# Sums of squares multiplied with a tile of 128 columns instead of a constant of two

## What is computed

```python
def rms_norm(x, g):
    xf = x.astype(jnp.float32)
    y = xf * lax.rsqrt(jnp.mean(xf * xf, axis=-1, keepdims=True) + EPS)
    return (y * g.astype(jnp.float32)).astype(x.dtype)

def first_block(x, ...):
    for layer in range(DEPTH):
        hn = rms_norm(x, norm_mix_g[layer])
        ...
        x = x + mix
        x = x + sq_relu_mlp(rms_norm(x, norm_mlp_g[layer]), mlp_w_up[layer], mlp_w_down[layer])
    return rms_norm(x, final_norm_g)
```

## Time and profile before

| | us |
|---|---|
| median of 3 runs | 850.53 (850.45 to 850.67) |
| the profiled execution | 849.28 |
| its span, first to last instruction | 847.5 |
| TensorE busy, matmuls | 842.2 |
| VectorE busy | 647.2 |
| ScalarE busy | 505.9 |
| GpSimd busy | 46.8 |

### The profile page before, as it was taken

The page is one execution under the profiler, slowest core; times in us unless marked ns, Lnnn a source line. Parts: engine busy times, 40 slices in busy tenths (PEclk is TensorE's granted clock), DMA queues, the critical chain, the costliest instruction groups (busy, mean ns, idle before and its releaser), DMA issues.

```text
span 847.5 us, 17537 instructions
## 1 busy us (share of the span) xinstructions
PE 842.2 (99%) x7184; PEld 822.4 (97%) x7184; DVE 647.2 (76%) x1229; ACT 505.9 (60%) x925; POOL 46.8 (6%) x63
## 2 busy tenths in 40 slices
PE   8999999999999999999999999999999999999998
PEld 7999999999999998999999999999999999999998
DVE  6978668898987697586667555566699889998873
ACT  5795777774435567578878444434456685444650
POOL 0000000000000127100000000021020000000000
PEclk9999999999999999999999999999999999999999
DMA  9927868788887824177757865526564424556541
GB/s 300 347 70 224 276 213 264 265 281 267 299 263 233 283 72 140 51 247 237 208 174 217 242 207 189 189 71 154 172 198 151 148 77 142 156 170 192 170 144 50
DMA packets 162865, 164.23 MB, mean 194 GB/s; under 512 B 16816, under 2 KB 159328, under 8 KB 162528
## 3 DMA queue, kind: packets, MB, share of 16 engines
q1 hardware_dynamic: 161696, 162.05, 60.6%
q10 hardware_dynamic: 1088, 1.05, 0.4%
HBM read 162.01 MB, written 2.91 MB: 195 GB/s over the span
## 4 chain that ended last, share of the span: by engine, by line
PE 97%; DVE 1%; DMA 1%; ACT 0%; SPq 0%; POOL 0%; issue 0%
PE ps L316 25%; PE ps L318 25%; PE ps L320 25%; PE ps L442 3%; PE ps L1594 2%; PE ps L1592 2%; PE ps L1596 2%; PE ps L459 2%; PE ps L1685 1%; PE ps L1687 1%; PE ps L1689 1%; PE ps L1643 1%; PE ps L1654 1%; PE ps L1634 1%; DMA raw<-in_rec_w_in_dram 1%; PE ps L1133 1%
## 5 line engine op out<-in xcount | busy, mean ns | idle before, releaser
L283 DVE TENSOR_TENSOR wl<-raw,wh 128x1024 fp32r<-128x1024 f32 x256 | 309.1, 1223 | 27.1 <-ACT wh L276 27.0
L316 PE MATMUL ps<-xh,wh 128*128 128x256 f32 x1136 | 319.1, 281 | 0.0
L318 PE MATMUL ps<-xl,wh 128*128 128x256 f32 x1136 | 315.1, 277 | 0.0
L320 PE MATMUL ps<-xh,wl 128*128 128x256 f32 x1136 | 315.0, 277 | 0.0
L276 ACT ACTIVATE wh<-raw 128x1024 fp32r<-128x1024 f32 x256 | 267.1, 1051 | 73.7 <-PE ps L320 66.0
L316 PEld LDWEIGHTS ps<-xh,wh 128*128 128x128 f32 x1136 | 213.3, 188 | 3.1 <-issue 1.2
L318 PEld LDWEIGHTS ps<-xl,wh 128*128 128x128 f32 x1136 | 213.8, 188 | 0.4 <-DVE xl L384 0.2
L320 PEld LDWEIGHTS ps<-xh,wl 128*128 128x128 f32 x1136 | 213.8, 188 | 0.0
L320 PE MATMUL ps<-hh,wl 128*128 128x256 f32 x512 | 141.3, 276 | 0.0
L316 PE MATMUL ps<-hh,wh 128*128 128x256 f32 x512 | 141.3, 276 | 0.0
L318 PE MATMUL ps<-hl,wh 128*128 128x256 f32 x512 | 141.3, 276 | 0.0
(11 more groups left out here) (365 smaller groups left out, 1396.4 us busy)
## 6 DMA issues: line engine op xcount, KB each, us to landing
raw<-in_w_in_dram SPq DMA_DIRECT2D x34, 1024.0 KB, 5.4
raw<-in_mlp_up_dram SPq DMA_DIRECT2D x32, 1024.0 KB, 5.5
raw<-in_mlp_down_dram SPq DMA_DIRECT2D x32, 1024.0 KB, 7.1
aw<-in_w_adaT_dram SPq DMA_DIRECT2D x24, 512.0 KB, 4.7
raw<-in_rec_w_in_dram SPq DMA_DIRECT2D x7, 1024.0 KB, 11.6
raw<-in_att_w_in_dram SPq DMA_DIRECT2D x6, 1024.0 KB, 5.5
raw<-in_rec_w_out_dram SPq DMA_DIRECT2D x4, 1024.0 KB, 5.9
raw<-in_att_w_o_dram SPq DMA_DIRECT2D x4, 1024.0 KB, 5.0
```

The lines of the kernel that those rows point to most:

```text
L283: e.tensor_tensor(parts_of(i)[1], raw_of(i), f32(parts_of(i)[0]), op=ALU.subtract).then_inc(S["wl"], 1)
L316: e.matmul(o, H[:, first + n], xh[:, k], start=start and n == 0, stop=False)
L318: e.matmul(o, H[:, first + n], xl[:, k], start=False, stop=False)
L320: ins = e.matmul(o, L[:, first + n], xh[:, k], start=False, stop=stop and n == len(ks) - 1)
```

## The change

The moving operand of the sums becomes ONES, a new tile of 128 x 128 filled with 1/1024 by GpSimd at the start, at an address of its own behind the other tiles. The first sum waits for that tile instead of the table, and the first spread, which reads the identity, gets the wait for the table. The results take 128 columns of a PSUM bank each where they took two; VectorE reads the first column of each.

```diff
+    ONES = place("ones", [128, 128], at=[228480])
...
     def rms_sum_pe(e, q, r):
         p = claim(q, AUX[0], (S["var"], r + 1))
         q.wait_ge(S["sqa"], 7 * (r + 1))
-        q.wait_ge(S["con"], 16)
-        e.matmul(p[:, 0:2], SQA[:, 0:128], cc("i1024"), start=True, stop=True)
-        e.matmul(p[:, 2:4], SQA[:, 128:256], cc("i1024"), start=True, stop=True).then_inc(closing(f"sum{r}", p), 1)
+        q.wait_ge(S["negh"], 2)
+        e.matmul(p[:, 0:128], SQA[:, 0:128], ONES[:], start=True, stop=True)
+        e.matmul(p[:, 128:256], SQA[:, 128:256], ONES[:], start=True, stop=True).then_inc(closing(f"sum{r}", p), 1)
 
     def rms_spread_pe(e, q, r):
         p = claim(q, AUX[1], (S["rs"], r + 1))
         q.wait_ge(S["rst"], r + 1)
+        q.wait_ge(S["con"], 16)
...
-        e.tensor_scalar(VAR, ps[f"sum{r}"][:, 0:4:2], EPS, None, op0=ALU.add).then_inc(S["var"], 1)
+        e.tensor_scalar(VAR, ps[f"sum{r}"][:, 0:256:128], EPS, None, op0=ALU.add).then_inc(S["var"], 1)
...
-                ins = e.matmul(p[:, 4 * i + 2 * b:4 * i + 2 * b + 2], acc[:, b * 128:b * 128 + 128], cc("i1024"),
+                ins = e.matmul(p[:, 256 * i + 128 * b:256 * i + 128 * b + 128], acc[:, b * 128:b * 128 + 128], ONES[:],
                                start=True, stop=True)
...
-        e.tensor_scalar(FV[:, 0:2], ps["fsum"][:, 0:4:2], EPS, None, op0=ALU.add).then_inc(S["fv"], 1)
+        e.tensor_scalar(FV[:, 0:2], ps["fsum"][:, 0:256:128], EPS, None, op0=ALU.add).then_inc(S["fv"], 1)
         q.wait_ge(S["fv"], 1)
-        e.scalar_tensor_tensor(FV[:, 2:4], FV[:, 0:2], EPS, ps["fsum"][:, 4:8:2], op0=ALU.mult,
+        e.scalar_tensor_tensor(FV[:, 2:4], FV[:, 0:2], EPS, ps["fsum"][:, 256:512:128], op0=ALU.mult,
                                op1=ALU.add).then_inc(S["fv"], 1)
...
             e.memset(NEGH[:], -0.5).then_inc(S["negh"], 1)
+            e.memset(ONES[:], 1.0 / 1024).then_inc(S["negh"], 1)
             e.memset(XRP[:, :, 0:3], 0.0).then_inc(S["pad"], 1)
```

## The result

| | before | changed |
|---|---|---|
| median, us | 850.60 (850.45 to 850.94) | 861.63 (861.15 to 862.70) |
| runs | 4 | 4 |
| span of the profiled execution, us | 847.5 | 859.6 |

The ratio is 1.0130, with a 95% interval of 1.0116 to 1.0143: 11.0 us slower. The forecast was 850.6 us, within 0.2% of no change, with a range of 849.5 to 851.8 and 0.05 for a loss over 0.2%. It was wrong.

What follows compares the result with a forecast made beforehand. The prediction took TensorE, on the chain for 97% of the span at full clock, as the bound. Matmuls 0.05, later sums 0 and memset with waits 0 were added to the 850.53 us median: 850.6 us, range 849.5 to 851.8.

Steps and rivals of the forecast that it cites:

- Part 1: The 28 fp32 passes of the sums: widening the moving operand from 2 to 128 columns adds only 0.05 us.
- rows 2: Trace rows around the 2-column sum in the norm ahead of the first MLP: 98.67 to 99.35, 0.68 us.
- rows 4: Trace rows around the final norm's eight passes with 2 columns: 552.13 to 553.25, 1.12 us.
- rows 3: Trace rows around the 128-column spread, two products after the first MLP's norm sum: 104.76 to 105.45, 0.69 us.
- The 0.08 us are given back at once: Inside a sum's group: the second call starts 0.08 us later, the next ordinary matmul follows that much sooner.
- rival B: At six sum groups the later starts are not given back: 0.08 us each remain, 0.48 us, 851.0 us; chance 0.08.
- Part 2: Behind the sums: each lands 0.11 us later, but idle time of its readers covers this; cost 0, at most 0.66 us.
- Part 3: Program start: GpSimd's new memset and the moved wait for the constants cost 0; without cover at most 0.31 us.
- A: At all 28 passes the columns are paid in full on top of the weight load: 853.5 us; chance 0.04.
- C: At the first sum, constants ordinarily land last and the sum is now free of them: up to -0.43 us, 850.1; chance 0.05.
- D: No set place: new tile's position or a shifted program start moves time beyond 0.2%; chance 0.03 (0.02 faster, 0.01 slower).

## Why the prediction was wrong, point by point

**What bounds the kernel.** Right: TensorE at the full clock, with no idle time. But "busy" was read as a fixed amount of work. The same matmuls take 113.3 or 117.8 ns each, and neither the busy share nor the clock tells which.

**Part 1, the price of the 28 passes: right as far as it went.** Forecast 0.68 to 0.70 us for the stretch of rows 2, measured 0.68; forecast 1.12 for that of rows 4, measured 1.13. The Trainium skill's rule for isolated matmuls (TensorE: Matmul & The Clock Gate, "Back-to-back issue gap"), by which the 28 passes would have cost 0.87 us more, the prediction's estimate, has no counterpart in these rows. The 107 ns for loading 128 columns, which the prediction puts into the same section of the Trainium skill, come from the formula in the next one, "LDWEIGHTS (loading the stationary operand)".

**The step that failed** is the sentence that made this comparison the whole of part 1: "So I compare like with like, from the start of the last ordinary matmul ahead of the group to the start of the second ordinary matmul behind it." The window ended at the second matmul behind, and everything further on was taken as unchanged. The term that was missing is 1488 + 312 + 1152 = 2952 matmuls, each of which starts about 4.4 ns further behind the one ahead of it, 13.0 us in the stretches behind three spreads (12.96 in the table of starts). The trace of before held the sign of it: the timeline a few rows past rows 2 goes from steps of 0.11 us to steps of 0.12, and past rows 3 back to 0.11. That a group changes the pace behind it was there to be read; that a wide sum would leave the other pace was not, since the trace had no such sum. The spreads of r = 1, 3 and 4, which the prediction took as its model of a wide sum, leave the pace opposite to the one they find. In a trace in which they always found the slow one, that looks like "128 columns leave the fast pace".

**"The 0.08 us are given back at once"** was right, and rival B (not given back) did not happen: in the changed kernel the ordinary matmul behind the sum starts at 98.83, 0.15 us after the second call at 98.68, where 0.14 was forecast and it had been 0.22.

**Part 2, the sum lands later: right.** VectorE waited for a sum twice, 1.5 us in all, where it had waited once, 1.1 us; the list of that line's waits after:

```profile
L368 DVE TENSOR_SCALAR tiny<-ps x5: 154/156/161, 15.0 to 424.3; 128x2 f32<-128x2 f32 x5
its engine sat idle before it (us, times) until:
  PE ps L335: 1.5, 2
```

TensorE didn't wait for a spread. The median durations of the sum's matmuls are 275 and 276 ns, as forecast.

**Part 3, memset and waits: right.** The memset took 0.20 us, at the place that was forecast:

```profile
0.73 0.12 POOL L2394 MEMSET negh<- 128x32 f32 x1 [0.29 <-POOLq L2483]
0.79 0.20 POOL L2395 MEMSET ones<- 128x128 f32 x1
5.00 0.42 POOL L2398 TENSOR_SCALAR sb_vec<-sb_vec 128x16 f32<-128x16 f32 x1 [3.95 <-DMA sb_vec<-in_vec_dram]
```

GpSimd still waits 3.95 us behind the memsets, so this cost nothing; the start of the program up to the spread of r = 1 is even 0.52 us shorter.

**Rivals.** A, the slower side, had 853.5 us with a chance of 0.04 and another mechanism, and its stretch of 1.1 us did not appear. C did not happen: the first sum again waited for VectorE's last addition, 0.50 us. D, "the change does something else than it says", had no mechanism and 0.01 on the slower side; the last sentence of the prediction names this outcome (stretches unchanged, medians over 1.7 us apart) as the one in which its argument is wrong. It is. A range built from this argument could not hold the time. A change at one place can set the pace of all that follows, so the range had to be as wide as thousands of matmuls times the difference of the two paces in the trace.

## What to carry to other kernels

When TensorE is busy throughout, measure the start-to-start time of the ordinary matmuls ahead of and behind every place that an edit touches, and multiply a difference of a few ns by the number of matmuls up to the next disturbance; the local cost of the edit says nothing about it. An edit at such a place can decide which pace follows: here it moved the time by 11 to 12 us at two addresses, and by no more than chance at a third. If two paces show up in a trace, try a short group of matmuls at the head of the long stretches, or another address for the tiles, before tuning the work inside them, and read the pace behind it, since a map found at one place did not hold at another.

## What the runs showed of the hardware that I had not expected

- A stream of fp32r matmuls, each of 256 columns with its own weights, has two steady paces at the granted clock of 1.00, 113.3 and 117.8 ns, 4%, and keeps either for over 1400 matmuls.
- A single load that came some 17 ns late (0.13 us after the one before it instead of 0.11), behind a VectorE result that was ready 42 ns ahead of it, was followed by the slow pace for the remaining 25 us of its stretch. No idle time shows it.
- At three of the norms the pace behind a group of fp32 passes followed from the group's kind and the pace ahead of it, without an exception in the 96 cases of the table. At the final pair the same kinds of operands did otherwise: the slow pace followed in all 15 traces.
- Tiles moved by 128 bytes changed what the spreads leave behind: the kernel before took 865.97 and 867.08 us at 352 and 96 modulo 512, 849.67 and 850.6 us at 480 and 224. Both paces occur at all four.
